# The input projection of a hybrid recurrent layer: plain column tiles, and Strassen products over pairs of them with the recurrent blocks beside the merge gates

## What is computed

```python
x += 0.5 * SwiGLU_1(RMSNorm(x))
h  = RMSNorm(x)
q, fpre, vin, gout, xr, yr, ga, gb = split(h @ w_in)      # eight parts of 1024 columns
f  = lb + (1 - lb) * sigmoid(fpre);  k = 1 - f;  q = silu(q)
# branch A, HGRN2: 8 heads, state 128x128, chunks of 64 tokens
S_t = diag(f_t) S_{t-1} + k_t v_t^T ;  o_t = S_t^T q_t
oA = RMSNorm_head(o) * o_norm * silu(gout)
# branch B, RG-LRU: 8 blocks of 128 channels
xc = causal_conv(xr, width 4);  r, i = sigmoid(block_diag(xc))
log_a = -8 r softplus(-lam);  h_t = a_t h_{t-1} + sqrt(1 - a_t^2) (i_t xc_t)
oB = h * gelu(yr)
m  = sigmoid(ga) * (oA @ w_a_up) + sigmoid(gb) * (oB @ w_b_up)
x += m @ w_out
x += 0.5 * SwiGLU_2(RMSNorm(x));  y = RMSNorm(x)
```

## Time and profile before

| | us |
|---|---|
| median of 3 runs | 2683.95 (2683.9 to 2684.68) |
| the profiled execution | 2683.54 |
| its span in the trace | 2681.7 |
| TensorE matmul busy | 2631.9 |
| VectorE busy | 1403.4 |
| ScalarE busy | 994.0 |
| FFN1, to the end of its last product | 0 to 752.6 |
| norm and first head's tiles | 752.6 to 810.0 |
| branch A | 810.0 to 1310.2 |
| merge A | 1310.2 to 1470.2 |
| branch B | 1470.2 to 1702.0 |
| merge B | 1702.0 to 1860.6 |
| output product | 1860.6 to 1953.6 |
| FFN2 and final norm | 1953.6 to the end |

### The profile page before, as it was taken

The page is one execution under the profiler, slowest core; times in us unless marked ns, Lnnn a source line. Parts: engine busy times, 40 slices in busy tenths (PEclk is TensorE's granted clock), DMA queues, the critical chain, the costliest instruction groups (busy, mean ns, idle before and its releaser), DMA issues.

```text
span 2681.7 us, 47409 instructions
## 1 busy us (share of the span) xinstructions
PE 2631.9 (98%) x18308; PEld 2568.4 (96%) x18308; DVE 1403.4 (52%) x2428; ACT 994.0 (37%) x1665; POOL 66.8 (2%) x76
## 2 busy tenths in 40 slices
PE   7999999999989999999999999999999999999997
PEld 6999999999989999999999999999999999999997
DVE  5755556566664444444311466423376665655665
ACT  4322322222365444444311566412352222322334
POOL 0000000000030000000000000000200000000002
PEclk8999999999999999999999999999999999999999
DMA  3111111111221111111111211313111111111112
GB/s 108 48 52 51 47 48 55 54 47 47 66 103 57 49 48 48 48 55 49 57 63 63 71 39 39 111 49 108 35 40 48 47 50 52 47 53 49 47 52 74
DMA packets 44493, 152.36 MB, mean 57 GB/s; under 512 B 5120, under 2 KB 9472, under 8 KB 43904
## 3 DMA queue, kind: packets, MB, share of 16 engines
q1 hardware_dynamic: 41680, 134.38, 16.5%
q10 hardware_dynamic: 2736, 16.91, 1.6%
HBM read 133.72 MB, written 17.55 MB: 56 GB/s over the span
## 4 chain that ended last, share of the span: by engine, by line
PE 93%; DVE 4%; ACT 2%; issue 1%; DMA 0%; POOL 0%; SPq 0%; DVEq 0%; ACTq 0%; POOLq 0%
PE banks L142 29%; PE banks L144 28%; PE banks L143 28%; PE banks L1563 1%; PE banks L1016 1%; PE banks L1026 1%; PE banks L1028 1%; PE banks L1052 1%; PE banks L1067 1%; PE banks L1007 1%; DVE f_blk_f L440 1%; PE banks L1009 1%; DVE y L274 1%; PE banks L1058 1%; DVE f_gt L842 0%
## 5 line engine op out<-in xcount | busy, mean ns | idle before, releaser
L142 PE MATMUL banks<-f_blk_hi,f_u_hi 128*128 128x258 f32 x2496 | 709.6, 284 | 13.2 <-DVE f_blk_lo L464 13.2
L143 PE MATMUL banks<-f_blk_lo,f_u_hi 128*128 128x258 f32 x2496 | 707.8, 284 | 0.0
L144 PE MATMUL banks<-f_blk_hi,f_u_lo 128*128 128x258 f32 x2496 | 707.0, 283 | 0.0
L142 PE MATMUL banks<-h_hi,w_hi 128*128 128x344 f32 x1728 | 572.6, 331 | 7.3 <-DVE h_lo L218 4.6
L144 PE MATMUL banks<-h_hi,w_lo 128*128 128x344 f32 x1728 | 553.3, 320 | 0.0
L143 PE MATMUL banks<-h_lo,w_hi 128*128 128x344 f32 x1728 | 553.2, 320 | 0.0
L142 PEld LDWEIGHTS banks<-f_blk_hi,f_u_hi 128*128 128x128 f32 x2496 | 473.6, 190 | 16.3 <-DVE f_blk_lo L464 9.7
L143 PEld LDWEIGHTS banks<-f_blk_lo,f_u_hi 128*128 128x128 f32 x2496 | 473.4, 190 | 0.1
L144 PEld LDWEIGHTS banks<-f_blk_hi,f_u_lo 128*128 128x128 f32 x2496 | 473.2, 190 | 0.0
L142 PEld LDWEIGHTS banks<-h_hi,w_hi 128*128 128x128 f32 x1728 | 326.2, 189 | 23.7 <-issue 20.2
L142 PE MATMUL banks<-f_hid_hi,f_u_hi 128*128 128x344 f32 x1056 | 341.9, 324 | 4.2 <-DVE f_hid_lo L688 3.3
(11 more groups left out here) (209 smaller groups left out, 2995.3 us busy)
## 6 DMA issues: line engine op xcount, KB each, us to landing
raw<-w_slabs SPq DMA_DIRECT2D x220, 512.0 KB, 3.6
x<-x_t SPq DMA_DIRECT2D x8, 516.0 KB, 7.5
x_kept<-x ACTq DMA_DIRECT2D x1, 4128.0 KB, 13.1
m_kept<-mt ACTq DMA_DIRECT2D x8, 516.0 KB, 2.7
m<-m_kept ACTq DMA_DIRECT2D x8, 516.0 KB, 9.0
x<-x_kept ACTq DMA_DIRECT2D x2, 2064.0 KB, 11.3
ss<-state_hgrn SPq DMA_DIRECT2D x8, 512.0 KB, 3.7
hgrn_s<-ss SPq DMA_DIRECT2D x8, 512.0 KB, 4.1
```

What stands on the lines that cost most here:

```text
L142: pe.matmul(out, wh, xh, start=start, stop=False, skip_group_check=chained)
L143: pe.matmul(out, wh, xl, start=False, stop=False, skip_group_check=chained)
L144: return pe.matmul(out, wl, xh, start=False, stop=stop, skip_group_check=chained)
```

## The change

**w_in as pairs.** Its 64 column tiles are put in another order. Group 0 is f, q, v and g of head 0, as plain products over four blocks of tokens (`plain_tensor`: 8 products of 48 matmuls of 258 columns). The 15 groups behind it are two pairs each, a pair being seven Strassen products of 24 matmuls of 258 columns. Groups 1 to 7 are (q, f) and (v, g) of heads 1 to 7. Groups 8 to 15 are (gate, gate) and (yr, xr), one group for a block of branch B.

**What runs beside them.** The HGRN core of head j-1 has its slots in the first pair of group j, for groups 1 to 8. The RG-LRU's block j-9 stands beside the first pair of groups 9 to 15 (`lru_pair`), the last block beside the up tiles.

**The norm** writes eight blocks of tokens for Strassen's products, high and low, instead of `h_hi` and `h_lo`. Parts of them (`EARLY`) are done while FFN1's last products run, the rest (`LATE`, B12, B22, T1 to T4) beside group 0.

**Kept in DRAM.** oA, oB and all 16 gate tiles (`oa_kept`, `ob_kept`, `sg_kept`); m no longer. The 16 up tiles stand at the end in one stage, `ups_*`, first the 8 of A and then the 8 of B, with oA, oB and one gate tile at a time loaded back by SyncE. x is written and read by SyncE's queue.

FFN1, the output product, FFN2 and the final norm keep their instructions.

Of the diff the core, first TensorE's order for a pair (`pair_weight` and `ffn_rows` name the weight and token block of product p):

```diff
+def pair_tensor(pe, k, s, j, c, after, first=False):
+    for p in range(7):
+        pair = c if p in (0, 2, 4, 6) else 1 - c
+        pe.wait_ge(s.unit_lo, seven(j, c, p + 1))
...
+        if p == 1:
+            if first:
+                pe.wait_ge(s.first_used, 6)
+            else:
+                pe.wait_ge(s.taken, one_of(j, c) - 1)
...
+        if p == 3:
+            pe.wait_ge(s.mixed, three_of(j, c, 1))
...
+        if p == 6:
+            pe.wait_ge(s.mixed, three_of(j, c, 2))
...
+        for g in range(2):
+            for kappa in range(KAPPAS):
+                last = three(pe, k.bank[2 * pair + g][:, 0:QW], pair_weight(s, p, kappa), ffn_rows(s, p, kappa, g),
+                             kappa == 0 and p in (0, 1, 3), kappa == KAPPAS - 1, chained=True)
+            if g:
+                last.then_inc(s.prod, 1)
+            after(2 * p + g)
```

VectorE's and ScalarE's order beside the second pair (v, g) of groups 1 to 7, and ScalarE's beside the first pair of groups 9 to 15. `ahead` splits units of the next pair, `three_of(j, c, n)` counts the mixes, `take` reads the fourth result straight from its bank:

```diff
+    def head_pair(j, first):
+        h = j - 1
+        affine(dve, k, s, j)
+        pair_low(dve, k, s, j, 1, 6)
+        cumulate(dve, k, s, j)
+        dve.wait_ge(s.vt_ready, j * 3)
+        mix(dve, k, s, j, 1, 0, s.vb[:, half(0)])
+        ahead(j + 1, 0, (0,))
+        keys(dve, k, s, j)
+        ahead(j + 1, 0, (1,))
+        sums(j + 1, 0, range(4))
+        finish_vector(dve, k, s, h, first)
+        queries(dve, k, s, j)
+        ahead(j + 1, 0, (2,))
+        dve.wait_ge(s.gated, j * 1)
+        mix(dve, k, s, j, 1, 1, s.sg[:, half(1)])
...
+    def head_pair(j):
+        h = j - 1
+        finish_square(act, k, s, h)
+        log_decay(act, k, s, j)
+        pair_high(act, k, s, j, 1, 6)
+        snap(act, k, s, j, 1, 0)
+        finish_log(act, k, s, h)
+        ahead(j + 1, 0, (0,))
+        exp_decay(act, k, s, j)
+        snap(act, k, s, j, 1, 1)
+        finish_rstd(act, k, s, h)
+        ahead(j + 1, 0, (1,))
...
+    def lru_pair(j):
+        b = j - 9
+        pair_high(act, k, s, j, 0, 6)
+        act.wait_ge(s.gelued, j - 8)
+        snap(act, k, s, j, 0, 0)
+        for p in (0, 1):
+            pair_high(act, k, s, j, 1, p)
+        snap(act, k, s, j, 0, 1)
+        lru_gates(act, k, s, b, 0)
+        snap(act, k, s, j, 0, 2)
+        lru_gates(act, k, s, b, 1)
+        for p in (2, 3):
+            pair_high(act, k, s, j, 1, p)
+        lru_gates(act, k, s, b, 2)
+        lru_decay(act, k, s, b)
...
+        take(j, 0, s.sgt[:, 0, half(1)], ACT.Sigmoid)
```

And the up tiles, TensorE and VectorE:

```diff
+def ups_tensor(pe, k, s):
+    for c in range(KT):
+        pe.wait_ge(k.slab_ready, c + 1)
+        if c == 0:
+            for b in range(4):
+                pe.wait_ge(s.oa_lo, 2 * b + 2)
+                for t in range(NT):
+                    if b == 0 and t == 0:
+                        pe.wait_ge(s.mixed, three_of(LAST, 1, 3))
...
+        for t in range(NT):
+            pe.wait_ge(s.up_used, 3 * c + t - 2)
+            product(pe, k, k.bank[t][:, 0:TG], c % 4, k.h_hi, k.h_lo, tg(t)).then_inc(s.up_ready, 1)
+            if c == 1:
+                lru_tensor(pe, k, s, KT - 1, t)
...
+def ups_vector(dve, k, s):
+    o = s.out
+    for m in (2, 3, 4, 5):
+        oa_low(dve, k, s, m)
+    ups_low(dve, k, s, 2)
+    for m in (6, 7):
+        oa_low(dve, k, s, m)
+    ups_low(dve, k, s, 3)
+    lru_conv(dve, k, s, GROUPS, range(4))
+    for u in range(UPS):
...
```

More of the change, by code:

```diff
@@ L192, in norm_behind_scalar @@
             norm_rstd(act, k, s, 0)
-    norm_hi(act, k, s, 0, 0)
     for m in range(KT):
[L195 to L198, removed]
         norm_square(act, k, s, 2, m)
[L200 to L229, removed]
+    norm_rstd(act, k, s, 1)
 def norm_add(eng, k, s, t, m):
@@ L746, in behind @@
             return
[L747 to L753, removed]
+        s.behind_scalar(act)
     def group(i, last=False):
@@ L1019, in output, with update @@
-    def output(h, n):
+        pe.matmul(k.bank[5][:, 0:P], s.ke[:, tok], s.qe[:, tok], start=True, stop=True).then_inc(s.sc_ready, 1)
+    def update(n, c):
+        if c:
+            pe.wait_ge(s.u_ready, h * 18 + (2 * n + 1))
+        else:
+            pe.wait_ge(s.kt_used, h * 9 + (n + 1))
+            wait(pe, s.u_used, h * 16 + 2 * n)
+        rows = slice(c * CHUNK, (c + 1) * CHUNK)
+        pe.matmul(k.bank[6][:, c * P:(c + 1) * P], s.kt[n % 2][rows, :], s.v[rows, n, :], start=True, stop=True)\
+            .then_inc(s.u_ready, 1)
@@ new lines, with core_means, core_turn @@
+MEAN_BANKS = (4, 5, 7)
+def core_means(pe, k, s, h):
+    pe.wait_ge(s.squared, h * 1 + 1)
+    pe.wait_ge(s.kt_used, h * 9 + 9)
+    for t in range(NT):
+        pe.matmul(k.bank[MEAN_BANKS[t]][:, 0:TG], k.ones_h[:, :], s.sq[:, tg(t)], start=True, stop=True)\
+            .then_inc(s.mean_ready, 1)
+def core_turn(pe, k, s, j, first=False):
+    if first:
+        pe.wait_ge(s.first_used, 8)
+    else:
+        pe.wait_ge(s.taken, one_of(j, -1))
+        pe.wait_ge(s.mixed, three_of(j, -1, 1))
+        pe.wait_ge(s.ln, j * 3 - 3)
+    pe.transpose(k.bank[5][0:DEC, 0:P], s.vb[:, SEQ:T], k.ident[:, :]).then_inc(s.vt_ready, 1)
+    for n in range(TILES):
+        last = pe.transpose(k.bank[6 + n // 4][:, (n % 4) * P:(n % 4 + 1) * P], s.vb[:, n * P:(n + 1) * P],
+                            k.ident[:, :])
+        if n % 4 == 3:
+            last.then_inc(s.vt_ready, 1)
@@ new lines, in core_scalar @@
+def core_scalar(act, k, s, h, n):
+    if 1 <= n < 9:
+        m = n - 1
+        act.wait_ge(s.u_ready, h * 18 + (2 * m + 2))
+        for c in range(2):
+            if m >= 2:
+                act.wait_ge(s.state, h * 17 + (2 * m - 1))
+            act.activation(s.ue[m % 2][:, c, :], k.bank[6][:, c * P:(c + 1) * P], ACT.Identity,
+                           scale=s.el[:, 2 * m + c:2 * m + c + 1]).then_inc(s.u_used, 1)
+    if n < 9:
+        rows = P if n < 8 else DEC
+        act.wait_ge(s.kt_ready, h * 9 + (n + 1))
+        if n >= 2:
+            act.wait_ge(s.u_ready, h * 18 + 2 * (n - 1))
+        act.activation(s.kt[n % 2][0:rows, :], k.bank[4][0:rows, 0:P], ACT.Copy).then_inc(s.kt_used, 1)
@@ new lines, in store_recurrent, with lru_tensor @@
+def store_recurrent(sp, k, s, b):
+    sp.wait_ge(s.ob_ready, b * 1 + 1)
+    sp.dma_start(k.ob_dram[bass.ds(b, 1)].rearrange("a p t -> p (a t)"), s.z[:, :]).then_inc(s.z_stored, 16)
+def lru_tensor(pe, k, s, b, t):
+    if t == 0:
+        pe.wait_ge(s.conv, b * 8 + 8)
+        pe.wait_ge(s.blocks_ready, b * 1 + 1)
+    wait(pe, s.gates_used, b * 6 + (2 if t == 2 else 0))
+    for c in range(2):
+        pe.matmul(k.bank[4 + 2 * c + t % 2][:, 0:TG], s.lw[:, c, :], s.xc[:, tg(t)],
+                  start=True, stop=True).then_inc(s.gates_ready, 1)
@@ new lines, in build @@
+    r = Region(slots, w2)
+    k.mid.update(u_hi=[], u_lo=[])
+    places = [(r, n) for n in range(7)] + [(Region(w2 + 7 * 4128 + 32, end), 7)]
+    for region, n in places:
+        k.mid.u_hi.append(region.put(f"mix_u_hi{n}", [P, 4 * P], F32R))
+        k.mid.u_lo.append(region.put(f"mix_u_lo{n}", [P, 4 * P], F32R))
+    nm_tiles = norm_tiles("nm", Region(r.at, w2))
+    k.mid.snap_t = [r.put(f"mix_snap{n}", [P, HW], F32) for n in range(3)]
+    k.mid.sum = sums("mix", r)
+    r = Region(w2, end)
```

1829 lines of the change are left out of this document (1004 added, 825 removed).

## The result

The changed kernel takes 2701.05 us (median of 4 runs, 2698.76 to 2702.67) against 2684.31 for the kernel before on the same chip (4 runs, 2683.9 to 2685.49). The ratio is 1.0061, with a 95% interval of 1.0044 to 1.0078: slower by 0.6%, where 24 us less were forecast. The profiled execution took 2702.14 us, its span is 2700.2.

What follows compares the result with a forecast made beforehand. TensorE's instruction time was taken as the bound. Products gain 73.9 us, new losses are 16.0 + 16.1 + 12.6 + 9.7 + 12, old losses of 16.2 go: -23.7, so 2660; range just under 2625 to 2706.

Steps and rivals of the forecast that it cites:

- The core's cover: HGRN core's slots: under a half product cut from about 2.0 to 1.44 us, the state chain fits, no stall; bounds 0, 43.
- The vector queue: HGRN groups 1 to 7, second pair: TensorE's seventh product waits for VectorE's late mix, 2.2 to 2.3 us a group.
- ScalarE's queue in the RG-LRU groups: Groups 9 to 15: TensorE's second product of the next pair waits 1.3 us for ScalarE's take freeing the bank.
- The convolution's stop: LRU groups 9 to 15: three convolution rounds end at 9.05, TensorE wants them at 8.65; stop of 0.4 to 0.5 us.
- The clock: Low clock after stops, 1.92 us a time: 6 to 7 in HGRN groups, 3 each at start and ups; 12 together.
- The start and the up tiles: First pair starts 62.1 us after FFN1, loss 16.0; up tiles lose 9.7 to oA's reload, convolution and the rest.
- table-load rival: Activation table switches in second pairs and LRU pairs each hold ScalarE a second 1.28 us: 45 more, 2705; chance 0.02.
- The slower rival: VectorE's and ScalarE's queues set the groups' period, 4.8 and 5.0 us over, 14 low clocks: up to 2720; chance 0.18.
- The rival on the product's pace: Smaller matmuls do not keep 0.1201 us beside the core; at 0.126 the time is 2692; chance 0.03.

Runs made afterwards that it cites:

- take-first run: Changed kernel with ScalarE's take of the bank ahead of weight units and shapes beside an RG-LRU block, three convolution rounds ahead of unit 6's low part: 2699.72 us.
- apart run: Kernel before with the second chunk's update issued behind the keys and scores, banks kept: 2722.68 us against 2683.26.
- serial run: Kernel before with the second chunk's update waiting for the first one's end, still directly behind it: 2718.52 us.

## Why the prediction was wrong

| term | predicted | measured |
|---|---|---|
| product, us per matmul | 0.1201 | 0.1202 |
| start, to the first pair | 62.1 and 3 of clock | 62.9 (64.34 less a half product of 1.44) |
| stop in a head's second pair | 2.2 to 2.3 | 2.24, first one 2.54 |
| low clock in these groups | 6 to 7 | 4.6 (three groups of 69.1) |
| head's group | 62.3 | 67.63 |
| group 8 in its window | 58.6 (60.04 less 1.44) | 63.74 |
| RG-LRU groups, seven | 319.5 | 322.4 |
| up tiles and output | 287.4 and 3 of clock | 290.9 |

One wording of the prediction is off and its sum is not: the 144 matmuls of 22.66 us are two whole column tiles, not two halves of one.

**The step that failed** is this sentence: "The HGRN core's small matmuls keep their number: a head takes 65.01 us with 288 plain matmuls (45.33), so 19.68 for core, means and turns; it moves under the products of another pair at the same price." They keep their number and not their price. The core costs 5.3 more per head, 7 x 5.3 + 5.1 for group 8 = 42 us, and 2660 + 42 = 2702 is the profiled execution (the other terms of the table come to less than 1 us together). The run with the updates side by side gives 34.9 of it back, or 40 by its groups without a low clock. Of the 0.62 a slot, 0.41 is the overlap of the two updates and 0.21 the steps around them, in front of the second pair of updates and at the outputs behind the first; the first number is shown by rows of four kernels, the cause of the second is not isolated.

It could have been seen. In the earlier trace rows the price of 19.68 is a difference and says nothing of what it is made of, and the trace of before had the row of four updates in 0.49 us. The diff has a wait of TensorE for itself (`u_ready` between the two updates) and one bank where there were two. I costed waits for other engines and passed over this one, since an engine's wait for itself looks free. And it never shows as idle time in the changed kernel, because keys and scores stand ahead of it; what it costs is that the second update runs alone.

**The core's cover** was argued rightly: the slack of 0.95 held against the 0.54 taken, and no slot waits on the state chain, not even with the shorter slot.

**The vector queue**: right in place, size and releaser, in all seven groups. The middle value, by back-to-back steps, was the right one of the bounds.

**ScalarE's queue in the RG-LRU groups**: right in place, 1.63 for 1.3. The convolution's stop, predicted at 0.4 to 0.5, was 1.35 in the group at 1414.52 and 0.16 in the next (1460.35 to 1460.51); the expectation of the take-first run had counted six of 1.35 where the trace shows one. The 2.9 us over are TensorE's own: of 309.81 busy, 98 products take 282.5, which leaves 3.9 a group for the gates where 3.5 were taken. What I did not see is that a second queue ended as late as the first, one pair on, so that its removal alone is worth nothing.

**The clock**: right in kind. 1.5 us were lost behind three of the seven stops, the granted clock being 0.63 over the 3.4 us shown above (in part at 1.2, in part at 2.4 GHz); 1.92 behind half of them was assumed. How near the forecast this came is luck: with the same seven stops it was five in the run with the updates side by side.

**The start and the up tiles**: right within 2.2 us (65.1 against 62.9, and 290.4 against 290.9), as was the table-load rival's small chance: every load is 1.28 with the next operation behind it.

**The rivals.** The slower rival gave a sign that came true and a mechanism that did not: its stops of 4.8 and 5.0 are 2.24 and 1.63. The rival on the product's pace was wrong too, since the pace held. No rival had more TensorE work in the core. The measured 2701 lies inside the range only thanks to the slower rival, and the forecast's own range, 2640 to 2676, missed it.

## What to carry to other kernels

When a change moves a group of instructions "as they are", read their rows on the engine itself before and ask what overlapped: the same count and mean duration with half the busy time meant two half-height matmuls beside each other. A change that needs one more PSUM bank may pay for it in such an overlap; look for two outputs moved into one bank and for a wait of an engine for its own result. And before a stop is put down as a gain, look for the next queue that ends close behind it: of the stops removed here only the one at the second up tile came off whole, and a wait beside it grew by 1.1; two left 0.35 and 0.6 behind, and two only moved.

## What the runs showed of the hardware

Two updates, matmuls over 64 rows each, in different halves of the array and with different banks, took 0.42 us together (before and together). A single one of them took 0.41 (the changed kernel and the apart run), and two with the second waiting for the first's result took 0.96 (the serial run: 0.55 us a slot in the whole time, 35.3 us over 64). The step from the scores to an update was 0.32 (the changed kernel and the apart run), to a product 0.14 (the kernel before). The low clock did not follow every stop: seven stops of the same 2.2 to 2.5 us, at even distances, had it behind three of them in the changed kernel (a group of 69.15 instead of 67.63) and behind five in the run with the updates side by side (64.17 instead of 62.61, granted clock 0.50 over the 3.4 us from 875.8 on).
